# Splitting the merge and output weights once, earlier, and keeping both parts in DRAM, in a hybrid decoder block on one core

## The reference

```python
gates = jax.nn.sigmoid(m_g.reshape(B_, T, N_BRANCH, D))
merged = (gates[:, :, 0] * (y_pool @ w_merge_pool[l])      # y_pool, y_hgrn, y_conv: 256 wide, y_diff: 512 wide
          + gates[:, :, 1] * (y_hgrn @ w_merge_hgrn[l])
          + gates[:, :, 2] * (y_conv @ w_merge_conv[l])
          + gates[:, :, 3] * (y_diff @ w_merge_diff[l]))
out = merged @ w_out[l]                                    # 1024 x 1024
x = x + gate[:, None] * rmsnorm(out, g_post[l])
```

## Time and profile before

| | |
|---|---|
| median of 3 runs | 2531.88 us (2531.22 to 2540.31) |
| the profiled execution's own time | 2534.88 us |
| its span (first to last instruction) | 2533.1 us |
| TensorE clock granted, mean | 0.959 of full speed |
| PE busy | 2274.4 us (90%), 11572 matmuls |
| PEld, DVE, ACT, POOL busy | 1871.5, 1434.6, 1144.1, 839.4 us |
| DMA moved | 564.75 MB, mean 223 GB/s |

### The profile page before, as it was taken

How to read it: one execution, slowest core, us unless ns; L and a number is a source line. 1 busy time by engine, 2 the same in 40 slices (tenths; PEclk the granted TensorE clock), 3 DMA queues, 4 the chain that set the end, 5 groups by cost and what they waited for, 6 DMA issues and landing times. The chain is left out here.

```text
span 2533.1 us, 35157 instructions
## 1 busy us (share of the span) xinstructions
PE 2274.4 (90%) x11572; PEld 1871.5 (74%) x11572; DVE 1434.6 (57%) x2638; ACT 1144.1 (45%) x2400; POOL 839.4 (33%) x739
## 2 busy tenths in 40 slices
PE   3698799998999889898999999999999966989898
PEld 2486677777777668687888888878888844767676
DVE  5676566655888777312766666445556334444442
ACT  3553455543544543422666666434434233434341
POOL 0113223223745645200222222124343225244353
PEclk7799999999999989999999999999999988999999
DMA  6799777757767667989464654588777676576581
GB/s 227 260 352 328 259 231 241 223 204 277 264 239 261 230 222 253 332 265 264 163 191 146 181 169 149 171 258 250 230 247 235 213 238 178 155 190 187 148 226 61
DMA packets 383963, 564.75 MB, mean 223 GB/s; under 512 B 32432, under 2 KB 248880, under 8 KB 382768
## 3 DMA queue, kind: packets, MB, share of 16 engines
q1 hardware_dynamic: 315248, 313.01, 42.0%
q10 hardware_dynamic: 68544, 249.59, 27.8%
HBM read 331.28 MB, written 231.21 MB: 222 GB/s over the span
## 5 line engine op out<-in xcount | busy, mean ns | idle before, releaser
L1682 PE MATMUL gb<-h_hi,w_both 128*128 128x512 f32 x1904 | 789.0, 414 | 87.2 <-ACT o L949 41.7
L1684 PE MATMUL gb<-h_hi,w_both 128*128 128x512 f32 x1904 | 757.7, 398 | 0.0
L1683 PE MATMUL gb<-h_lo,w_both 128*128 128x512 f32 x1904 | 756.7, 397 | 0.0
L1682 PEld LDWEIGHTS gb<-h_hi,w_both 128*128 128x128 f32 x1904 | 366.9, 193 | 171.2 <-issue 91.7
L1684 PEld LDWEIGHTS gb<-h_hi,w_both 128*128 128x128 f32 x1904 | 365.7, 192 | 81.2
L1683 PEld LDWEIGHTS gb<-h_lo,w_both 128*128 128x128 f32 x1904 | 367.7, 193 | 67.1
L949 ACT ACTIVATE o<-gb 128x512 f32<-128x512 f32 x272 | 161.4, 594 | 372.5 <-PE gb L1684 308.0
L809 POOL TENSOR_TENSOR C_prob<-C_prob,C_cf 128x512 f32<-128x512 f32 (+3 forms) x160 | 156.9, 1005 | 506.1 <-DVE C_cf L1358 492.1
L1014 ACT ACTIVATE C_prob<-C_sc,C_negm 128x512 f32<-128x512 f32 (+3 forms) x320 | 198.5, 622 | 246.6 <-DVE C_negm L1336 239.9
L1250 DVE TENSOR_TENSOR o<-gb,o 128x512 f32<-128x512 f32 x204 | 140.3, 688 | 231.0 <-PE gb L1684 220.0
L1240 DVE TENSOR_TENSOR w_both<-w,w_both 128x512 fp32r<-128x512 f32 x170 | 142.1, 836 | 171.5 <-ACT w_both L922 171.1
(11 more groups left out here) (230 smaller groups left out, 3722.6 us busy)
## 6 DMA issues: line engine op xcount, KB each, us to landing
wS_scratch<-w_both ACTq DMA_DIRECT2D x238, 512.0 KB, 4.4
w_both<-wS_scratch ACTq DMA_DIRECT2D x238, 512.0 KB, 4.3
w<-in_w_in_dram SPq DMA_DIRECT2D x68, 512.0 KB, 5.2
gT_scratch<-o SPq DMA_DIRECT2D x128, 256.0 KB, 4.6
D_gate<-gT_scratch SPq DMA_DIRECT2D x32, 1024.0 KB, 9.8
pT_scratch<-o SPq DMA_DIRECT2D x80, 256.0 KB, 4.2
C_qt<-qB_scratch SPq DMA_DIRECT2D x128, 128.0 KB, 3.4
C_ks<-kT_scratch SPq DMA_DIRECT2D x48, 256.0 KB, 5.7
```

What stands on the lines that cost most here:

```text
L1682: mm(to, hi[:, k, :], h_hi[j][:, k, :], start=(fresh and k == 0), stop=False, skip_group_check=True)
L1683: mm(to, hi[:, k, :], h_lo[j][:, k, :], start=False, stop=False, skip_group_check=True)
L1684: last = mm(to, lo[:, k, :], h_hi[j][:, k, :], start=False, stop=(k == KH - 1), skip_group_check=True)
```

## The change

Three things are changed together.

1. **The splits move into the trunk and are kept.** The merge weights (10 row chunks of 128 x 1024) and w_out (8 chunks) are cut into 36 blocks of 128 x 512. Block k is loaded by SP in slot 283 + 5k into an idle staging tile, copied to its high part by ACT and subtracted by DVE in slot 286 + 5k, and stored by SP in slot 287 + 5k: the merge parts to wmS (two DMAs with 512-byte pieces), the output parts to woS. The last block's slot is 461. merge_and_output then loads high and low parts together (wm_both, 10 KB a partition in one DMA; wo_both, 8 KB), and its splits of weights are gone: 32 on ACT and 32 on DVE of 128x1280, 8 on ACT and 8 on POOL of 128x1024. A weight load now waits for the end of the merge step that last used the buffer (`merged_done`), since TensorE reads from the tile that is loaded.
2. **Gates are asked for ahead of weights** in SP's merge steps; the loads of w_out are spread over the eight steps of group 0.
3. **Two output blocks ahead of the last tiles.** TensorE does k = 0 to 5 of block 0 and of block 1, then waits for m_lo of steps 6 and 7, then does k = 6 and 7 of both.

The diff, cut to its core:

```diff
+SPLITS, APART, BLOCKS = 286, 5, 36
+def block_at(slot, offset):
+    k, r = divmod(slot - SPLITS - offset, APART)
+    return k if r == 0 and 0 <= k < BLOCKS else None
@@ trunk, SP
+            def load_block(k):
+                sp.wait_ge(wlo, KEPT + max(0, k - 1))
...
+                sp.dma_start(block_in[k % 2], src).then_inc(w2_loaded[k % 2], 16)
+            def store_block(k):
+                sp.wait_ge(wlo, KEPT + k + 1)
+                row, half = k // 2, k % 2
+                if row < YC:
+                    for part in range(2):
+                        sp.dma_start(wmS[4 * half:4 * half + 4, :, part, row, :].rearrange("d p c -> p d c"),
+                                     block_both[k % 2][:, part, :].rearrange("p (d c) -> p d c", c=P)).then_inc(block_stored[k % 2], 16)
+                else:
+                    sp.dma_start(woS[row - YC, :, :, half * TG:half * TG + TG], block_both[k % 2]).then_inc(block_stored[k % 2], 16)
@@ trunk, SP's slots: after the loads of w1 and w2
+                k = block_at(n, -3)
+                if k is not None:
+                    load_block(k)
+                k = block_at(n, 1)
+                if k is not None:
+                    store_block(k)
@@ trunk, ACT (called in slot n with block_at(n, 0), behind load_weights)
+            def high_block(k):
+                act.wait_ge(w2_loaded[k % 2], 16 * (NU // 2 + k // 2 + 1))
+                if k >= 2:
+                    act.wait_ge(block_stored[k % 2], 16 * STORES[k - 2])
+                a(block_both[k % 2][:, 0, :].bitcast(F32R), block_in[k % 2], ACT.Copy).then_inc(whi, 1)
@@ trunk, DVE (called in slot n with block_at(n, 0), behind add_out)
+            def low_block(k):
+                dve.wait_ge(whi, KEPT + k + 1)
+                tt(block_both[k % 2][:, 1, :].bitcast(F32R), block_in[k % 2], block_both[k % 2][:, 0, :], ALU.subtract).then_inc(wlo, 1)
@@ merge_and_output, SP
             def load_wm(n, d):
                 if not (isinstance(n, int) and n < 2):
-                    sp.wait_ge(wm_hi_ready, n - 1)
-                    sp.wait_ge(wm_lo_ready, n - 1)
-                for w, (c0, c1) in zip(w_merge, BRANCH_CHUNKS):
-                    sp.dma_start(wm_stage[d % 2][:, c0:c1, :], w[0, :, d * P:(d + 1) * P].rearrange("(k p) n -> p k n", p=P)).then_inc(wm_loaded[d % 2], 16)
+                    sp.wait_ge(merged_done, 4 * (n - 1))
+                sp.dma_start(wm_both[d % 2][:, :, :, :].bitcast(F32).rearrange("p l k c -> p (l k c)"),
+                             wmS[d].rearrange("p l k c -> p (l k c)")).then_inc(wm_loaded[d % 2], 16)
...
                     if not (last and d + 2 >= KD):
+                        load_gates(n + 2, (d + 2) % KD, at if d + 2 < KD else at_next)
                         load_wm(n + 2, (d + 2) % KD)
-                        load_gates(n + 2, (d + 2) % KD, at if d + 2 < KD else at_next)
-                    if first and d + NW < KD:
-                        load_wo(d + NW)
+                    if first:
+                        load_wo(d)
@@ merge_and_output, POOL
-                    if first:
-                        pool.wait_ge(wo_hi_ready, d + 1)
-                        tt(wo_lo[:, d, :], wo_in[d % NW][:, :], wo_hi[:, d, :].bitcast(F32), ALU.subtract).then_inc(wo_lo_ready, 1)
@@ merge_and_output, DVE (its split_wm is gone)
-                    if d + 1 < KD:
-                        split_wm(n + 1, d + 1)
@@ merge_and_output, ACT (its split_wm and the copies to wo_hi are gone)
-                        split_wm(g, n + 1, d + 1)
                         sigmoids(g, n + 1, d + 1)
@@ merge_and_output, PE
-                    pe.wait_ge(wm_lo_ready, n + 1)
+                    pe.wait_ge(wm_loaded[d % 2], 16 * (KD // 2 * g + d // 2 + 1))
...
                 if first:
-                    pe.wait_ge(wo_lo_ready, KD)
+                    pe.wait_ge(wo_loaded, 16 * KD)
+                for b in range(2):
+                    if not first:
+                        pe.wait_ge(scaled, TB * g + b - 1)
+                    if b == 0:
+                        pe.wait_ge(m_lo_ready, KD * g + KD - 2)
+                    for half in range(2):
+                        for k in range(KD - 2):
+                            output(g, b, half, k)
+                pe.wait_ge(m_lo_ready, KD * g + KD)
+                for b in range(2):
+                    for half in range(2):
+                        for k in range(KD - 2, KD):
+                            done = output(g, b, half, k)
+                    done.then_inc(p_done, 1)
+                for b in range(2, TB):
+                    pe.wait_ge(scaled, TB * g + b - 1)
+                    for half in range(2):
+                        for k in range(KD):
+                            done = output(g, b, half, k)
                     done.then_inc(p_done, 1)
```

More of the change, by code:

```diff
@@ L255, in trunk @@
         KEEPS = [len(range(r, KEPT, RING)) for r in range(RING)]
+        STORES = [sum(2 if b // 2 < YC else 1 for b in range(k % 2, k + 1, 2)) for k in range(BLOCKS)]
         product_done, copied, summed = sem("product_done"), sem("copied"), sem("summed")
@@ L751, in _ @@
             mixers_over(1)
+            for j in range(2):
+                sp.wait_ge(block_stored[j], 16 * STORES[BLOCKS - 2 + j])
             for b in range(4):
@@ L1898, in _, with merge_and_output @@
                     transposes(i)
-BRANCH_CHUNKS = ((0, 2), (2, 4), (4, 6), (6, 10))
-YC = 10
-def merge_and_output(nc, x, w_merge, w_out, gT, yT, post_d, out):
+def merge_and_output(nc, x, wmS, woS, gT, yT, post_d, out):
     with ExitStack() as ctx:
@@ L1917, in merge_and_output @@
         GB = 4
-        wo_stage = sb("wo_stage", [P, D])
-        wo_hi = sb("wo_hi", [P, KD, D], F32R)
-        wo_lo = sb("wo_lo", [P, KD, D], F32R)
-        wm_stage = [sb(f"wm_stage{j}", [P, YC, P]) for j in range(2)]
-        wm_hi = [sb(f"wm_hi{j}", [P, YC, P], F32R) for j in range(2)]
-        wm_lo = [sb(f"wm_lo{j}", [P, YC, P], F32R) for j in range(2)]
+        square = sb("square", [P, D])
+        wo_both = sb("wo_both", [P, KD, 2, D], F32R)
+        wm_both = [sb(f"wm_both{j}", [P, 2, YC, P], F32R) for j in range(2)]
         y_stage = [sb(f"y_stage{j}", [P, TG]) for j in range(2)]
@@ L2225, in body @@
+                            mm(mb[b][:, :], wm_both[d % 2][:, 0, k, :], y_lo[:, k, :], start=False, stop=False)
+                            done = mm(mb[b][:, :], wm_both[d % 2][:, 1, k, :], y_hi[:, k, :], start=False, stop=(k == c1 - 1))
                         done.then_inc(merged_done, 1)
                 if first:
-                    pe.wait_ge(wo_lo_ready, KD)
-                for b in range(TB):
-                    n = TB * g + b
-                    if not (first and b < 2):
-                        pe.wait_ge(scaled, n - 1)
+                    pe.wait_ge(wo_loaded, 16 * KD)
```

91 lines of the change are left out of this document (34 added, 57 removed).

## The result

The changed kernel takes 2540.97 us (median of 20 runs, 2532.96 to 2546.04), the kernel before 2534.44 in the same series (20 runs). The ratio is 1.0026, 95% interval 1.0017 to 1.0034: 0.3% slower, where 2% faster was forecast. The profiled execution took 2538.77 us, its span is 2537.0 us (2533.1 before), the mean granted clock 0.964; it moved 618.23 MB instead of 564.75.

The account below looks back on a forecast made before the run. It took the trunk as bound by a gapless TensorE and merge steps by a ring through POOL, not TensorE; 2534.88 - 19 - 1 - 15 - 17 + 2 = 2484.9, for the median 2482, rounded to 2481 us; range 2470 to 2508.

Parts of the forecast that it names:

- trunk: Trunk's second half: 36 added splits beside a gapless TensorE cost 2 us (bounds 0 to 17), their stores zero.
- group 0's output starts: Group 0's merge, DMA-bound at 8.5 us a step: output starts at 2128.5 instead of 2147.55, 19 us gained.
- group 0's output: Block 0 of group 0: the 1.43 us wait for m_lo goes, less a new wait: 1 us gained.
- merges of groups 1 to 3: Merge steps go from the ring's pace to TensorE's 6.82 us: 5.0 us gained per group, 15 in all.
- outputs of groups 1 to 3: Output blocks: waits for m_lo of 6.81 and 7.14 us and low clock go, 1.5 us new waits: net 17 gained.
- Does the DMA follow?: Merge steps: doubled weights 3.2 us plus gates 2.7 make 5.9 in TensorE's 6.82; weight load lands in 5 to 6.
- The ring and TensorE's pace: Merge steps: the POOL, m_hi, m_lo, multiplications loop falls from 7.62 to 6.43 us, so TensorE's 6.82 sets the pace.
- Two blocks ahead: Outputs: 72 matmuls, 16.3 us, instead of 36 (8.2) cover m_lo of step 7, needed 15.0 to 15.6 after the merge.
- `scaled` of block 0: Outputs of groups 1 to 3: block 2 waits for block 0's scaling chain, 0.5 us each, 1.5 in all.
- The idle ahead of group 0's output: Before group 0's output: TensorE still idles over 10 us, now ended by a DMA, at about 2128; lower clock stays.
- The DMA is the pace: Rival, 17%: transfers run at 324 GB/s, merge steps take 7.3 us, group 0 hardly shortens; total 2508.
- Each merge step waits out its weight load: Rival, 5%: with one step of time for the load, steps take 10.2 us; decides from an 8.6 landing; total 2560.

Follow-up runs that it names:

- gate_rows: The changed kernel with the four gates of a step side by side in their scratch tensor (8 KB rows, same bytes and order): 2488.78 us, ratio 0.9831.
- half_weights: The changed kernel, loading only the high half of a step's merge weights from step 2 on (0.66 instead of 1.31 MB): 2494.77 us, ratio 0.9853.
- gate_rows_three_buffers: The changed kernel with the gates of a step side by side and a third buffer for merge weights: 2484.27 us, ratio 0.9814.
- two_blocks_gate_rows: The kernel before with two output blocks ahead of the last tiles and the gates of a step side by side: 2501.33 us, ratio 0.9885.
- w_out_in_two: gate_rows_three_buffers with w_out waited for in two parts, row blocks 6 and 7 only ahead of the first output's last tiles: 2474.91 us, ratio 0.9765.

## Why the prediction was wrong

Profile against profile, by the terms of the forecast's sum:

| term | forecast | measured |
|---|---|---|
| trunk | +2 | +6.2 |
| group 0's output starts | -19 | -1.0 |
| group 0's output | -1 | -1.4 |
| merges of groups 1 to 3 | -15 | +11.3 |
| outputs of groups 1 to 3 | -17 | -11.2 |
| sum | -50 | +3.9 |

The outcome, within 0.5% of no change, had been given 2%.

**The step that failed is "Does the DMA follow?", and in it the 2.7 us for a step's gates.** It took the 149 GB/s of the earlier trace rows for the weights' 512-byte rows and the 324 for gates, and so gave the gates 390 GB/s. The packet sizes and times say the reverse: the gates are the slower transfer. In the merge of group 1 they ran at 248 GB/s, 4.2 us a step, with stretches at 180 to 187; the 3.2 us for the doubled weights, at 409, were nearly right (3.4). gate_rows shows that this is the cause: with the gates' layout alone changed, 52 us come back, and group 0's output starts 19.4 us earlier than before, where 19 was forecast. From the wrong term followed 5.9 us of DMA a step (7.3 measured, above TensorE's 6.82), most of the landing (5 to 6 us forecast, 9.0 measured, 6.9 in gate_rows), group 0's 8.5 us a step and thus 18 of its 19 us, and the late y (2276.00, 12.7 us after group 1's merge ended at 2263.3, instead of 8), which cost most of the 5.8 missing in the outputs.

**A second, smaller fault** is in the same step: that a load with one step of time "fits with about 1 us left". Even with fast gates the third buffer takes 7.2 us off the three merges.

**The ring and TensorE's pace** were right: POOL's add is 2.40 us, and half_weights and gate_rows_three_buffers run merges of 55.4 to 55.8 and 54.6 us, where 54.5 to 55 was forecast; two_blocks_gate_rows, which keeps the splits and has fast gates, stays at 59.7. **Two blocks ahead**: right, 16.6 us alone, where the sum has 17 and 1 for group 0. `scaled` of block 0 costs 0.4 us in each group, for which 0.5 was taken. **The idle ahead of group 0's output** stayed over 10 us with a DMA behind it, as said, but at 2152.73 and not at about 2128. **The trunk**: mis-sized. The trunk from the attention on is 5.4 us longer, about 3.6 of it for the splits, where 2 and zero for the stores were taken; the other 0.8 of the 6.2 had come up before the attention. A slip of reading without effect on the sum: the 102 us given as group 0's merge include the 10.16 ahead of its output, the merge itself takes 92.5.

**The rivals.** "The DMA is the pace" named the right resource, but with 324 GB/s it still gave 2508; at the 283 to 303 GB/s of these steps, 2.36 MB take 7.8 to 8.3 us, above the old pace of 7.5. "Each merge step waits out its weight load" named the right wait, with a landing of 9.0 where it decides from 8.6, but it is the smaller cause: a third buffer brought 9.8 us, the layout 52. Both were at work together, and in the merges their prices add up.

The Trainium skill, DMA: Bandwidth & Descriptors, "Specifications", puts the core's share at about 358 GB/s. In w_out_in_two group 0's merges ran at 411 GB/s with a share of 1.00 for 66 us, so this program was not held to 358:

```profile
2052.00:2118.00 66.00, 56.84 (x233) 45.21 (x234) 26.56 (x43) 22.28 (x21) 25.33 (x14) 0.95 1.00 411
```

I had used 149 GB/s against that page's rule that rows of 512 bytes suffice for the line rate. That window was two thirds gates by bytes; the other one, with 1296 packets of 512 bytes and 383 larger ones (299 of 2 KB, 84 of 4 KB), ran at 324. By their own time, 27 and 31 ns, the 512-byte packets stood at 303 and 264 GB/s, well above 149. No window here holds 512-byte rows alone, so the rule is not tested, but my contradiction is withdrawn. The same page's "Latency and other measured facts" has a rule close to this case: copies whose partitions' rows lie 4 or 8 MiB apart in DRAM run at about half the full rate (at 512 KiB apart still nearly in full), and a padding of 4 KiB or a contiguous layout restores it. It gives nothing for rows 8 KB apart. Here 8 KB between rows and 8 MB between gates did it together: in the merge of group 1 a gate packet took 132 ns instead of 86 to 90. It leaves the mechanism unproven, and so do these runs.

## What to carry to other kernels

Before a rate read from a window is given to a transfer, count the packets of each size in it, and look at more than one window: a busy DMA at a low rate may be another tensor's fault, and a scratch tensor of one's own can be laid out so that what is loaded together lies together. When work is cheapened by doubling its bytes, look first at the slowest transfer that shares the queue. In an in-order queue a load with a free buffer must not stand behind one that waits for TensorE.
